# Down projection of a fused decoder layer: the signs of its block products, and two of four weight sums made by an accumulating DMA

## The reference

```
y = conv_ffn(h, w_up, conv_w, conv_b, w_down)
#   u = h @ w_up;  uc = conv_b + causal depthwise conv of width 3 over u;  a, val = split(uc)
#   (silu(a) * val) @ w_down            w_down: 5632 x 2048, activations: 256 x 5632
h_res = h_res + rmsnorm(y, post_ffn_g)
```

## Time and profile before

| | |
|---|---|
| median of 3 runs | 1199.63 us (1199.42 to 1199.9) |
| the profiled execution | 1199.66 us |
| its span, first to last instruction | 1197.9 us |
| mean granted TensorE clock | 0.998 |
| PE / DVE / ACT / POOL busy | 1186.6 / 800.2 / 653.7 / 377.2 us |
| down projection, first matmul to last | 961.2 to 1190.6 us |
| DMA in the stage | 44.60 MB from 955 on, mean 184 GB/s |

### The profile page before, as it was taken

One profiled execution on the slowest core, in us unless ns is written; L12 is line 12 of the kernel. 1 busy time (PEld: TensorE's weight loads), 2 busy tenths in 40 slices (PEclk: granted clock), 3 DMA queues, 4 the chain that ended last, 5 costly groups with the idle time before them and its releaser, 6 DMA issues.

```text
span 1197.9 us, 23215 instructions
## 1 busy us (share of the span) xinstructions
PE 1186.6 (99%) x8870; PEld 1131.3 (94%) x8870; DVE 800.2 (67%) x1140; ACT 653.7 (55%) x993; POOL 377.2 (31%) x183
## 2 busy tenths in 40 slices
PE   9999999999999999999999999999999999999997
PEld 8999999999999999999999999999999988888876
DVE  6865555464555346766666677666665699999998
ACT  7544545455784447545444444444454466666665
POOL 1233333333424442444444444444444310000000
PEclk9999999999999999999999999999999999999999
DMA  9655554554436664565565655556565556666562
GB/s 340 199 159 158 141 159 140 160 141 141 141 124 202 190 202 126 173 189 173 184 189 165 191 183 182 181 172 190 175 192 179 172 176 207 216 193 211 192 203 79
DMA packets 172906, 212.45 MB, mean 177 GB/s; under 512 B 6704, under 2 KB 158640, under 8 KB 172720
## 3 DMA queue, kind: packets, MB, share of 16 engines
q1 hardware_dynamic: 172416, 210.32, 57.2%
q10 hardware_dynamic: 432, 1.34, 0.3%
HBM read 209.53 MB, written 2.10 MB: 177 GB/s over the span
## 4 chain that ended last, share of the span: by engine, by line
PE 94%; DVE 4%; DMA 1%; ACT 0%; issue 0%; SPq 0%; DVEq 0%; ACTq 0%
PE psum L509 72%; PE psum L2090 10%; PE psum L2119 5%; DVE w_lo L573 2%; PE psum L1726 2%; PE psum L1957 1%; PE psum L1786 1%; DMA raw<-in_w_first 1%; PE psum L1812 0%; PE psum L2047 0%; PE psum L1890 0%; PE psum L1908 0%; DVE proj L1577 0%; PE psum L1813 0%; DVE proj L1685 0%; PE psum L1903 0%
## 5 line engine op out<-in xcount | busy, mean ns | idle before, releaser
L509 PE MATMUL psum<-a_hi,w_hi 128*128 128x258 f32 (+1 forms) x2360 | 673.8, 286 | 0.8 <-ACT temp L767 0.8
L509 PE MATMUL psum<-a_lo,w_hi 128*128 128x258 f32 (+1 forms) x2360 | 673.8, 286 | 0.0
L509 PE MATMUL psum<-a_hi,w_lo 128*128 128x258 f32 (+1 forms) x2360 | 670.0, 284 | 0.0
L493 POOL TENSOR_TENSOR w_lo<-raw,w_hi 128x1024 fp32r<-128x1024 f32 x144 | 361.5, 2510 | 576.6 <-ACT w_hi L489 576.6
L489 ACT ACTIVATE w_hi<-raw 128x1024 fp32r<-128x1024 f32 x307 | 322.4, 1058 | 328.1 <-PE psum L509 323.1
L509 PEld LDWEIGHTS psum<-a_hi,w_hi 128*128 128x128 f32 x2360 | 448.3, 190 | 6.1 <-issue 3.9
L509 PEld LDWEIGHTS psum<-a_lo,w_hi 128*128 128x128 f32 x2360 | 448.4, 190 | 0.0
L509 PEld LDWEIGHTS psum<-a_hi,w_lo 128*128 128x128 f32 x2360 | 446.0, 189 | 0.1
L493 DVE TENSOR_TENSOR w_lo<-raw,w_hi 128x1024 fp32r<-128x1024 f32 x164 | 216.2, 1320 | 249.4 <-ACT w_hi L489 247.3
L1518 DVE SCALAR_TENSOR_TENSOR proj<-proj,par 128x256 f32<-128x256 f32 x88 | 109.5, 1245 | 37.5 <-ACT proj L986 37.5
L567 ACT ACTIVATE w_hi<-raw 128x1024 fp32r<-128x1024 f32 x84 | 89.1, 1061 | 45.6 <-PE psum L2090 35.2
(11 more groups left out here) (264 smaller groups left out, 993.4 us busy)
## 6 DMA issues: line engine op xcount, KB each, us to landing
raw<-in_w_up SPq DMA_DIRECT2D x176, 512.0 KB, 3.6
raw<-in_w_in SPq DMA_DIRECT2D x88, 512.0 KB, 4.1
raw<-in_w_down SPq DMA_DIRECT2D x88, 512.0 KB, 4.3
raw<-in_w_out SPq DMA_DIRECT2D x32, 512.0 KB, 3.8
raw<-in_w_first SPq DMA_DIRECT2D x7, 512.0 KB, 10.9
xT<-in_features SPq DMA_DIRECT2D x3, 544.0 KB, 7.6
out<-proj SPq DMA_DIRECT2D x6, 256.0 KB, 2.4
temp<-in_post_ffn_g ACTq DMA_DIRECT2D x1, 1024.0 KB, 4.6
```

The source lines that it names most:

```text
L493: eng.tensor_tensor(w_lo[:, j % SPLIT, :], raw[:, j, :], w_hi[:, j % SPLIT, :], ALU.subtract)\
L509: mm = pe.matmul(psum[:, bank + m, 0:t1 - t0], w[:, j % SPLIT, cols], a[:, k, t0:t1], start=(k == 0 and step == 0), stop=(k == KT - 1 and ...
```

## The change

For each seven pair a third chunk, `sums`, is loaded ahead of `b1` and `b2`: the right halves [B12, B22] of both row blocks, in rows of 2 KB. When it has landed, GpSimd issues a DMA that reads `b1`'s rows, [B11, B12], from HBM again and adds them onto it in SBUF (`accum_op`), so that it holds [B12 + B11, B22 + B12], the second unit. It waits for one such DMA before it issues the next. ScalarE and VectorE wait for it (`w_summed`). On VectorE the 1024-wide operation is gone; the other two are now B22 + (B12 + B11) into `b1`'s right half and B21 + that into `w_last`. The signs move to the activation sums (`pair_sum`) and to `prepare` and `prepare_whole`. In the dense stretch `differences` part 0 stood ahead of the plain pair's first split (`between`); now it always stands behind it. The chunks are numbered anew, 104 of them in place of 88, in the same 8 slots. And the activations of a plain pair are split by one 512-wide operation in place of two 256-wide ones, on ScalarE and on VectorE, so ScalarE waits until both units of the plain pair two before are used.

```diff
@@ -151,15 +152,17 @@
         for place, kind in enumerate(kinds):
             form, at = FORM_AT[half][n] if kind == "S" else (0, 0)
-            pairs.append(Pair(half, kind == "S", n, unit, 2 * len(pairs), plain, seventh, form, at, place))
+            ahead = 1 if kind == "S" else 0
+            pairs.append(Pair(half, kind == "S", n, unit, chunk + ahead, chunk, plain, seventh, form, at, place))
             unit += 4 if kind == "S" else 2
+            chunk += 2 + ahead
             plain += 0 if kind == "S" else 2
             seventh += 1 if kind == "S" else 0
...
+        def loads(pr):
+
+            rows = [slice((2 * pr.pair + n) * P, (2 * pr.pair + n + 1) * P) for n in range(2)]
+            cols = slice(pr.half * CHUNK, (pr.half + 1) * CHUNK)
+            whole = [(pr.chunk + n, w_down[0, rows[n], cols]) for n in range(2)]
+            if not pr.seven:
+                return whole
+            right = w_down[0, 2 * pr.pair * P:2 * (pr.pair + 1) * P, cols.start + BANK:cols.stop]
+            return [(pr.sums, right.rearrange("(n p) c -> p n c", p=P))] + whole
+
+        def last_unit(c):
+
+            pr = max((o for o in DOWN if o.sums <= c), key=lambda o: o.unit)
+            if not pr.seven:
+                return pr.unit + c - pr.chunk
+            return pr.unit + (1, 2, 0)[c - pr.sums]
...
-            return (raw_of(pr.chunk + 1), w_diff[:, 0:CHUNK], raw_of(pr.chunk), w_diff[:, CHUNK:])[n]
+            return (raw_of(pr.chunk + 1), raw_of(pr.sums), raw_of(pr.chunk), w_last)[n]
...
+        def plain_user(pr):
+
+            return max(o.unit for o in DOWN if not o.seven and o.plain == pr.plain - 4)
...
         def unit_hi(eng, pr, n):
             u = pr.unit + n
@@ -562,8 +584,10 @@
                 await_landed(eng, pr.chunk + n)
             elif n == 0:
                 await_landed(eng, pr.chunk + 1)
+            elif n == 1:
+                eng.wait_ge(w_summed, 16 * (pr.seventh + 1))
             else:
-                eng.wait_ge(diffs_ready, 2 * pr.seventh + min(n, 2))
+                eng.wait_ge(diffs_ready, 2 * pr.seventh + n - 1)
             eng.activation(w_unit(w_hi, u)[:, 0:src.shape[1]], src, ACT.Copy).then_inc(hi_ready, 1)
...
-            for c in range(2 * len(DOWN)):
-                kt, half = chunk_rows(c)
-                if c >= RAW:
-                    u = unit_of(c - RAW)
-                    if u < SPLIT:
-                        sp.wait_ge(lo_ready(u), UP1 // 2 + u // 2 + 1)
+            for pr in DOWN:
+                for c, src in loads(pr):
+                    if c < RAW:
+                        sp.wait_ge(lo_ready(c), UP1 // RAW * 4 + (c // 2 - 3))
+                    elif last_unit(c - RAW) < SPLIT:
+                        sp.wait_ge(lo_ready(last_unit(c - RAW)), UP1 // 2 + last_unit(c - RAW) // 2 + 1)
                     else:
-                        sp.wait_ge(d_w_ready, u - SPLIT + 1)
-                else:
-                    sp.wait_ge(lo_ready(c), UP1 // RAW * 4 + (c // 2 - 3))
-                sp.dma_start(raw_of(c), w_down[0, kt * P:(kt + 1) * P, half * CHUNK:(half + 1) * CHUNK])\
-                    .then_inc(raw_landed[c % RAW], 16)
+                        sp.wait_ge(d_w_ready, last_unit(c - RAW) - SPLIT + 1)
+                    dst = raw_of(c)
+                    if len(src.shape) == 3:
+                        dst = dst.rearrange("p (n c) -> p n c", n=2)
+                    sp.dma_start(dst, src).then_inc(raw_landed[c % RAW], 16)
...
+            for pr in DOWN:
+                if pr.seven:
+                    await_landed(pool, pr.sums)
+                    if pr.seventh > 0:
+                        pool.wait_ge(w_summed, 16 * pr.seventh)
+                    pool.dma_start(raw_of(pr.sums), w_down[0, 2 * pr.pair * P:(2 * pr.pair + 1) * P,
+                                                           pr.half * CHUNK:(pr.half + 1) * CHUNK], accum_op=ALU.add)\
+                        .then_inc(w_summed, 16)
...
-            def down_hi(pr, n):
-                kt = 2 * pr.pair + n
-                act_e.wait_ge(act_made, kt + 1)
-                copy(d_hi[:, (pr.plain + n) % 4, :], act[:, kt * seq:(kt + 1) * seq]).then_inc(d_hi_ready, 1)
+            def down_hi(pr):
+                act_e.wait_ge(act_made, 2 * pr.pair + 2)
+                if pr.plain >= 4:
+                    act_e.wait_ge(chunk_used, UP1 + plain_user(pr) + 2)
+                copy(d_pair(d_hi, pr), act_pair(pr)).then_inc(d_hi_ready, 1)
...
-                    if not pr.seven and pr.unit >= SPLIT:
-                        down_hi(pr, n)
+                    if not pr.seven and pr.unit >= SPLIT and n == 0:
+                        down_hi(pr)
...
-                a, b, op = ((rows[:, :, 0], rows[:, :, 2], ALU.add), (sums[:, :, 0], rows[:, :, 1], ALU.subtract),
+                a, b, op = ((rows[:, :, 0], rows[:, :, 2], ALU.subtract), (rows[:, :, 1], sums[:, :, 0], ALU.subtract),
                             (rows[:, :, 1], rows[:, :, 0], ALU.subtract), (rows[:, :, 3], sums[:, :, 1], ALU.subtract))[n]
                 dve.tensor_tensor(sums[:, :, n], a, b, op).then_inc(sums_made, 1)
...
-            def down_lo(pr, n):
-                kt, at = 2 * pr.pair + n, (pr.plain + n) % 4
-                dve.wait_ge(d_hi_ready, pr.plain + n + 1)
-                dve.tensor_tensor(d_lo[:, at, :], act[:, kt * seq:(kt + 1) * seq], d_hi[:, at, :],
-                                  ALU.subtract).then_inc(d_ready, 1)
+            def down_lo(pr):
+                dve.wait_ge(d_hi_ready, pr.plain // 2 + 1)
+                dve.tensor_tensor(d_pair(d_lo, pr), act_pair(pr), d_pair(d_hi, pr), ALU.subtract).then_inc(d_ready, 1)
...
             def differences(pr, part):
 
-                b1, b2 = raw_of(pr.chunk), raw_of(pr.chunk + 1)
+                b1, b2, both = raw_of(pr.chunk), raw_of(pr.chunk + 1), raw_of(pr.sums)
                 if part == 0:
                     for c in (pr.chunk, pr.chunk + 1):
                         await_landed(dve, c)
+                    dve.wait_ge(w_summed, 16 * (pr.seventh + 1))
+                    dve.tensor_tensor(b1[:, BANK:], b2[:, BANK:], both[:, 0:BANK], ALU.add).then_inc(diffs_ready, 1)
+                else:
                     if pr.seventh > 0:
                         dve.wait_ge(d_w_ready, max(o.unit for o in DOWN if o.seven and o.unit < pr.unit) + 4 - SPLIT)
-                    right = raw[:, pr.chunk % RAW:pr.chunk % RAW + 2, BANK:]
-                    dve.tensor_tensor(w_diff[:, 0:CHUNK].rearrange("p (n c) -> p n c", n=2), right,
-                                      b1.rearrange("p (n c) -> p n c", n=2), ALU.subtract).then_inc(diffs_ready, 1)
-                else:
                     dve.wait_ge(diffs_ready, 2 * pr.seventh + 1)
-                    dve.tensor_tensor(b1[:, BANK:], b2[:, BANK:], w_diff[:, 0:BANK], ALU.subtract).then_inc(diff_step, 1)
-                    dve.wait_ge(diff_step, pr.seventh + 1)
-                    dve.tensor_tensor(w_diff[:, CHUNK:], b2[:, 0:BANK], b1[:, BANK:], ALU.subtract)\
-                        .then_inc(diffs_ready, 1)
+                    dve.tensor_tensor(w_last, b2[:, 0:BANK], b1[:, BANK:], ALU.add).then_inc(diffs_ready, 1)
...
-                for n, (dst, a, b) in enumerate(((four, six, one), (three, seven, four), (four, five, four))):
+                for n, (dst, a, b, op) in enumerate(((four, one, six, ALU.subtract), (three, seven, four, ALU.add),
+                                                     (four, five, four, ALU.subtract))):
                     if n > 0:
                         dve.wait_ge(prep_step, 4 * half + n)
-                    dve.tensor_tensor(dst, a, b, ALU.add).then_inc(prep_step, 1)
...
-                dve.tensor_tensor(whole, product(half, 1), three, ALU.add).then_inc(prep_step, 1)
+                dve.tensor_tensor(whole, product(half, 1), three, ALU.subtract).then_inc(prep_step, 1)
...
-                between = p > 0 and DOWN[p - 1].seven and following and following.seven and not pr.seven
-                if between:
-                    differences(following, 0)
                 for n in range(4 if pr.seven else 2):
                     if n == 3 and pr.next_form:
                         form_lo(pr.next_form)
                     if pr.unit + n >= SPLIT:
                         unit_lo(dve, pr, n)
-                    if not pr.seven and pr.unit >= SPLIT:
-                        down_lo(pr, n)
-                    if following and following.seven and not pr.seven and not (between and n == 0):
+                    if not pr.seven and pr.unit >= SPLIT and n == 0:
+                        down_lo(pr)
+                    if following and following.seven and not pr.seven:
                         differences(following, n)
...
             def plain_chunk(pr, n, done=None):
                 await_unit(pr.unit + n)
-                pe.wait_ge(d_ready, pr.plain + n + 1)
+                pe.wait_ge(d_ready, pr.plain // 2 + 1)
```

34 lines of the change are left out of this document (15 added, 19 removed).

## The result

| | before | changed |
|---|---|---|
| median | 1199.77 us (1199.42 to 1200.38, 4 runs) | 1213.91 us (1210.07 to 1215.25, 4 runs) |
| ratio | | 1.0113, 95% interval 1.0101 to 1.0126 |
| profiled execution, span | 1199.66, 1197.9 us | 1215.25, 1213.4 us |

A forecast was written before the change was run, and what follows sets the result against it. TensorE, busy 99% of the span, was taken as the bound, so only its stalls and the end could gain: 1199.66 - 1.2 (VectorE stalls) - 0.2 (tail) = 1198.3 us, range 1197.4 to 1212.0.

The forecast's parts named there:

- VectorE's relief: Dense stretch of the down projection: VectorE's period falls from 10.71 to 9.5 us, under TensorE's 10.20; stalls go, -1.2 us.
- W: Time an accumulating DMA on GpSimd's queue takes from issue to landing, taken as 7.0 us.
- The 63%: Busy share of the DMA queue in the down stage, from which it was taken as not saturated.
- I expect it to fit: DMA traffic in a dense period: 308 GB/s, or 360 counting the destination read, against 345 to 404 reached.
- rival (b): Narrow misses at the first seven pair or at the DMA ceiling give back the gain: 1199.6 us; chance 0.10.
- No cost: SyncE's 16 more loads in the eight-slot ring: it lasts 16.3 us instead of 20.4, plain chunks keep several us of lead.
- What W may be: Longest W without a TensorE stall at the dense stretch's third seven pair: 8.7 to 11.2 us, middle 10.
- W may be 8.1 us: Limit for W at the first seven pair, where GpSimd is free only at 964.85 and the sum needed at 972.9.
- Rival (a): Accumulation late, W above about 10 us: VectorE, then TensorE wait at up to 15 seven pairs; 1208 to 1227 us; chance 0.31.
- The tail: End of the kernel after the last seven pair: merged activation splits save 0.1 to 0.2 us, taken as -0.2 us.

The follow-up runs named there:

- e2: The changed kernel with the accumulation cut to 128 of 1024 columns, 64 KB: 1199.06 us, ratio 0.9996.
- e4: The changed kernel with only the right half (256 KB) accumulated and B12 + B11 made on VectorE: 1198.96 us, ratio 0.9996.
- g1: The kernel of e4 again, unchanged, in more rounds (11 runs): 1198.88 us, ratio 0.9993 against the kernel before.
- e3: The changed kernel without any accumulating DMA; VectorE and ScalarE wait for the third chunk itself: 1199.44 us, ratio 0.9998.
- f3: The kernel before with only the merged activation splits of a plain pair, on ScalarE and VectorE: 1200.74 us, ratio 1.0009.
- e1: The changed kernel with GpSimd's DMA copying instead of adding, same bytes from HBM and same waits: 1200.56 us, ratio 1.0005.
- f4: The changed kernel with each accumulation replaced by two plain 512 KB copies on the same queue: 1213.13 us, ratio 1.0136.
- g2: The changed kernel with VectorE's two additions moved behind the seven pair's own first splits, whole accumulation kept: 1199.96 us, ratio 1.0002.
- f2: The changed kernel with the third chunk loaded two chunks earlier, ahead of the plain pair before it: 1213.8 us, ratio 1.0116.
- g3: The changed kernel with SyncE waiting after a seven pair's third load until the accumulation has landed: 1235.93 us, ratio 1.0302.

## Why the prediction was wrong

- **VectorE's relief, -1.2 us: right in mechanism, about half in size.** Where the accumulation does no harm 0.6 to 0.9 us are gained (e2, e4, g1), 0.3 in e3; each interval holds 1. The pieces of the dense stretch are 5.46 us and even (5.44 in the best case). The rest is likely to have gone to the merged splits, which alone cost 1 us (f3); the prediction had priced them at a gain. That they are the rest is not shown.
- **W = 7.0 us: the step that failed.** Its terms were 4.4 for a plain load, 1.3 for reading the destination, 1.3 for "a plain load in flight beside it". Plain loads themselves rose to 6.4 us. Beside each of the five longest accumulations there is not one load but six in all, four or five at a time: three that were sent just ahead, its own pair's `b1` and `b2` among them, and three of the next places. The 63% that W was sized by was the share of the kernel before; with the change the queue is 65.6 + 20.9 = 86.5% busy. A term for the destination was right to have: adding costs 1.87 times a copy's engine time. The size that decides was the largest, 12.1 us, not the median, 7.9. Why accumulations with five or six loads beside them land in 6.6 to 8.0 us at most other pairs is open; the five have three loads in flight when they are issued, most others one or two.
- **"I expect it to fit": wrong, and it is the same error.** 308 or 360 GB/s against 345 and 404 compared means over a period. The Trainium skill (page Collectives: The Full Stack, section The bandwidth ceiling) states for the adding step of a collective that it needs two source reads and so runs at half the rate of the copying one. For this DMA e1 and f4 bear that out, with 1.87 and 2.0 x 20.9/22.0 = 1.90 copies for one accumulation. Counted so, the 360 was the true load, and in the burst of 995 to 1000 the engines are full at 298 GB/s of counted bytes. The prediction named the rule and let it change nothing but rival (b); it should have changed W.
- **"No cost" for SyncE: right for the ring** (e3), wrong for what stands around an accumulation: three loads go out from 988.1 to 989.6, the accumulation at 990.22, and three loads more by 995.9.
- **What W may be, 8.7 to 11.2 us: it held as a range.** TensorE has five waits of over 0.5 us for a weight's low part, and they follow the accumulations of 11.25, 10.60, 10.91, 12.11 and 9.43 us; none follows that of 9.98 or one of 8.94 or less. The limit is one for both transfers: at the pair of 9.43 us the third chunk took 8.68, above the 6.9 that was allowed for it, together 18.1 us where 15.6 were there; that is 2.5 over, and TensorE stood still for 2.6. I worked the limit out for the dense stretch, but the five of over 9.9 us are exactly those of a seven pair behind two plain pairs, which I had not looked at by itself.
- **"W may be 8.1 us" for the first pair: met, and not free.** It landed in 7.81 us and the plain pair's weights were in time. But the limit counts only the next unit. VectorE stood still for 3.62 us and lost the lead that it needed ten microseconds later, which cost 0.9 us at 983.61.
- **Rival (a), chance 0.31: right in place; its price came out by luck.** It asked for VectorE before the first addition, the plain pair's split behind it, and TensorE waiting for that; all of that is in the trace. It gave +10 us for a W of 10.5 and +29 for 11.7 at 15 pairs. By its rule, what exceeds 10 us at each pair, the landings measured give 1.25 + 0.60 + 0.91 + 2.11 = 4.9 us, and not the 9.5 that TensorE waited for weights: the limit is not 10 at every pair, and a slow third chunk counts as much. It also left out the low clock behind a stall, 3.2 us here, and the late activations, 1.4. It took the place in VectorE's order as given; g2 shows that this place could be moved, and that the loss goes with it.
- **The tail, -0.2 us:** not there. From the end of the last matmul to the end of the span it is 6.9 us before, 7.0 after, and 7.1 in e2, where nothing stalls.

## What to carry to other kernels

Price an accumulating DMA as two copies in the DMA engines, and judge a queue by its fullest 5 us and its slowest landing, not by a period's mean. Before a wait is put on an engine that works in order, list what stands behind it: the same accumulation cost 14 us ahead of a neighbour's split and nothing two splits later. Count the lead of the waiting engine too: a wait that nobody needs at once can be paid later. Loading earlier (f2) and holding others back (g3) did not help here, where the queue was full and worked in order; they only chose who was late.

## What the runs showed of the hardware

- One accumulating DMA of 512 KB took 1.87 times the DMA engines' time of the same copy (20.9% against 11.2%, e1), and landed as two copies do (5.5/7.9/12.1 us against 5.6/7.9/11.4, f4).
- GpSimd is busy 0.86 us (862 ns) to issue an accumulating DMA of 512 KB, 0.53 us (530 ns in e1) for the same as a copy; it was 862 ns for 64 KB too (e2).
- An accumulation of 64 KB still needs 5.1 us in the median, where one of 512 KB with no later load beside it needs 6.4 (g3).
- Stalls of 2.14 and 1.80 us on TensorE were each followed by about eight matmuls at nearly half speed (granted clock 0.66 in 1030 to 1035); one of 2.56 us was not.
